# GLA groups of a hybrid scan layer: the products of both 64-channel heads side by side in the instruction order

## What is computed

```
def step(s, blk):                       # one chunk of 32 tokens
    qb, kb, vb, gb = blk
    b = jnp.cumsum(gb, axis=-2)
    b_last = b[..., -1:, :]
    q_dec = qb * jnp.exp(b)
    k_inv = kb * jnp.exp(-b)
    k_tail = kb * jnp.exp(b_last - b)
    att = jnp.where(lower_tri, jnp.einsum("bhik,bhjk->bhij", q_dec, k_inv), 0.0)
    o = jnp.einsum("bhij,bhjv->bhiv", att, vb) + jnp.einsum("bhik,bhkv->bhiv", q_dec, s)
    s_new = jnp.swapaxes(jnp.exp(b_last), -1, -2) * s + jnp.einsum("bhjk,bhjv->bhkv", k_tail, vb)
    return s_new, o
```

## Time and profile before

| | |
|---|---|
| median of 3 runs | 1610.77 us (1608.57 to 1614.6) |
| profiled execution, its own time | 1610.87 us |
| its span, first to last instruction | 1609.1 us |
| PE busy | 1465.1 us, 91% of the span |
| DVE, ACT, POOL busy | 704.9, 513.9, 85.3 us |
| mean granted clock of TensorE | 0.959 of full speed |
| DMA | 178.09 MB, mean 111 GB/s |

### The profile page before, as it was taken

How to read it: one execution, slowest core, us unless ns; L and a number is a source line. 1 busy time by engine, 2 the same in 40 slices (tenths; PEclk the granted TensorE clock), 3 DMA queues, 4 the chain that set the end, 5 groups by cost and what they waited for, 6 DMA issues and landing times.

```text
span 1609.1 us, 18385 instructions
## 1 busy us (share of the span) xinstructions
PE 1465.1 (91%) x7701; PEld 1191.7 (74%) x7701; DVE 704.9 (44%) x891; ACT 513.9 (32%) x715; POOL 85.3 (5%) x90
## 2 busy tenths in 40 slices
PE   3589999999999998999999999998776999999994
PEld 1377777777779998777777677887565887888883
DVE  2324333333335784553154436666673333423245
ACT  2233421122212545434243325555233222122220
POOL 3100000000000000000011101110000000000000
PEclk9999999999999999999989799999887999999997
DMA  9525446555434664550111101213421332333221
GB/s 297 188 79 157 151 151 185 175 162 159 150 125 126 169 177 122 165 183 17 40 53 40 27 27 40 53 53 105 131 79 51 107 99 86 92 105 91 86 73 52
DMA packets 201937, 178.09 MB, mean 111 GB/s; under 512 B 6642, under 2 KB 166912, under 8 KB 201856
## 3 DMA queue, kind: packets, MB, share of 16 engines
q1 hardware_dynamic: 192000, 139.14, 29.9%
q0 software_dynamic: 9856, 37.78, 7.1%
HBM read 174.81 MB, written 2.10 MB: 110 GB/s over the span
## 4 chain that ended last, share of the span: by engine, by line
PE 83%; DVE 7%; ACT 5%; issue 4%; DMA 1%; POOL 1%; SPq 0%; ACTq 0%; DVEq 0%; POOLq 0%
PE ps L1524 24%; PE ps L1525 23%; PE ps L1526 23%; PE ps L1548 2%; PE ps L1806 2%; ACT w_hi L648 1%; PE ps L1838 1%; PE ps L1836 1%; ACT hfull L664 1%; DVE w_lo L1034 1%; PE ps L1564 1%; PE ps L1555 1%; DVE stats L1049 1%; PE ps L1809 1%; PE ps L1821 1%
## 5 line engine op out<-in xcount | busy, mean ns | idle before, releaser
L1524 PE MATMUL ps<-h_hi,w_lo 128*128 128x512 f32 (+2 forms) x1136 | 403.5, 355 | 21.3 <-DVE h_lo L1069 16.2
L1034 DVE TENSOR_TENSOR w_lo<-w_raw,w_hi 128x2048 fp32r<-128x2048 f32 (+3 forms) x113 | 250.5, 2219 | 379.5 <-ACT w_hi L648 379.3
L1525 PE MATMUL ps<-h_lo,w_hi 128*128 128x512 f32 (+2 forms) x1136 | 398.1, 350 | 0.0
L1526 PE MATMUL ps<-h_hi,w_hi 128*128 128x512 f32 (+2 forms) x1136 | 397.7, 350 | 0.0
L648 ACT ACTIVATE w_hi<-w_raw 128x2048 fp32r<-128x2048 f32 (+3 forms) x113 | 209.5, 1855 | 547.5 <-PE ps L1526 546.3
L1524 PEld LDWEIGHTS ps<-h_hi,w_lo 128*128 128x128 f32 (+1 forms) x1136 | 217.7, 192 | 60.1 <-DVE h_lo L1069 17.2
L1526 PEld LDWEIGHTS ps<-h_hi,w_hi 128*128 128x128 f32 (+1 forms) x1136 | 217.2, 191 | 30.3
L1525 PEld LDWEIGHTS ps<-h_lo,w_hi 128*128 128x128 f32 (+1 forms) x1136 | 217.7, 192 | 28.6
L1524 PE MATMUL ps<-h_hi,half_lo 128*128 128x512 f32 (+1 forms) x272 | 108.1, 398 | 3.3 <-DVE gate L1377 3.3
L1525 PE MATMUL ps<-h_lo,half_hi 128*128 128x512 f32 (+1 forms) x272 | 103.7, 381 | 0.0
L1526 PE MATMUL ps<-h_hi,half_hi 128*128 128x512 f32 (+1 forms) x272 | 103.2, 379 | 0.0
(11 more groups left out here) (198 smaller groups left out, 1901.9 us busy)
## 6 DMA issues: line engine op xcount, KB each, us to landing
w_raw<-ffn_w_in SPq DMA_DIRECT2D x132, 512.0 KB, 5.3
ada_block<-w_ada POOLq DMA_DIRECT2D x36, 1024.0 KB, 6.0
w_raw<-ffn_w_out SPq DMA_DIRECT2D x60, 512.0 KB, 4.1
half_raw<-w_mix_in SPq DMA_DIRECT2D x48, 256.0 KB, 3.3
w_raw<-w_mix_out SPq DMA_DIRECT2D x12, 512.0 KB, 4.8
w_raw<-w_mix_in SPq DMA_DIRECT2D x8, 512.0 KB, 4.2
w_raw<-ffn_w_out SPq DMA_DIRECT2D x12, 256.0 KB, 3.9
xl<-x SPq DMA_DIRECT2D x4, 512.0 KB, 11.1
```

What stands on the lines that cost most here:

```text
L1034: nc.vector.tensor_tensor(lo, raw, hi.bitcast(F32), ALU.subtract).then_inc(s_lo[s], 1)
L1524: nc.tensor.matmul(dst, s_low, m_high, start=start, stop=False)
L1525: nc.tensor.matmul(dst, s_high, m_low, start=False, stop=False)
L1526: return nc.tensor.matmul(dst, s_high, m_high, start=False, stop=stop)
```

## The change

For GLA groups, a function `attention_pair` takes the place of the two calls of `attention`. It goes tile by tile: the KINV product of head one, that of head two, the 64x64 product of head one, that of head two. `updates` exchanges its two loops, so that the heads alternate there too (for HGRN groups, with one head, it stays what it was). `attention_pair` stands directly ahead of `updates`, after the dense products that used to stand between the first head's attention and the updates. On DVE the first head's mask moves behind `tails` (direction 0) or behind `scans` (direction 1).

```diff
+            def attention_pair(g, d):
+                (hd, _, _), _ = heads_of(g)
+                pe.wait_ge(s_qdec, n2(g, d))
+                pe.wait_ge(s_kinv, n2(g, d))
+                pe.wait_ge(s_tail, n2(g, d))
+                pe.wait_ge(s_kt, n2(g, d))
+                pe.wait_ge(s_am, max(ATT[g, d, hd] - 1, 0))
+                a0, b0 = (0, HALF) if d == 0 else (HALF, 0)
+                for tile in range(TL):
+                    c = tile * P
+                    for hd, p0, pn in heads_of(g):
+                        nc.tensor.matmul(ps[:, att_bank(g, hd), c:c + P], KINV[d][p0:p0 + pn, c:c + P],
+                                         QDEC[d][p0:p0 + pn, c:c + P], start=True, stop=True, skip_group_check=True)
+                    for hd, p0, pn in heads_of(g):
+                        ins = nc.tensor.matmul(ps[a0:a0 + HALF, att_bank(g, hd), c + b0:c + b0 + HALF],
+                                               TAILX[d][p0:p0 + pn, c + a0:c + a0 + HALF],
+                                               QDEC[d][p0:p0 + pn, c + b0:c + b0 + HALF], start=True, stop=True,
+                                               skip_group_check=True)
+                        if tile == TL - 1:
+                            ins.then_inc(s_att, 1)
...
             def updates(g, d):
                 pe.wait_ge(s_kt, n2(g, d))
-                for hd, p0, pn in heads_of(g):
-                    v = slice(hd * P, (hd + 1) * P)
-                    for j in range(5):
+                for j in range(5):
...
+                    for hd, p0, pn in heads_of(g):
+                        v = slice(hd * P, (hd + 1) * P)
...
                 turn_tails(g, 0)
-                attention(g, 0, first)
+                if not gla:
+                    attention(g, 0, first)
                 if gla_next:
                     dense(nxt, "gate0")
                 else:
                     dense_lat(nxt, "f0")
+                if gla:
+                    attention_pair(g, 0)
                 updates(g, 0)
-                if gla:
-                    attention(g, 0, second)
...
                     turn_tails(g, 1)
-                    attention(g, 1, first)
                     gla_z(nxt, 0)
                     dense(nxt, "gate1")
+                    attention_pair(g, 1)
                     updates(g, 1)
-                    attention(g, 1, second)
                     gla_z(nxt, 1)
```

More of the change, by code:

```diff
@@ L1410, in _ @@
                     forget(g, 1)
-                mask(g, 0, first)
+                if not gla:
+                    mask(g, 0, first)
                 scans(g, 1)
@@ L1416, in _ @@
                 decayed(g, 1)
-                states(g, 0)
-                tails(g, 1)
+                if gla:
+                    tails(g, 1)
+                    mask(g, 0, first)
+                    states(g, 0)
+                else:
+                    states(g, 0)
+                    tails(g, 1)
                 if gla_next:
@@ L1431, in _ @@
                     forget(nxt, 0)
-                mask(g, 1, first)
+                if not gla:
+                    mask(g, 1, first)
                 if gla_next:
@@ L1812, in attention @@
                 ins.then_inc(s_att, 1)
+            def attention_pair(g, d):
[18 more added lines that the diff above has]
+                            ins.then_inc(s_att, 1)
             def updates(g, d):
                 pe.wait_ge(s_kt, n2(g, d))
-                for hd, p0, pn in heads_of(g):
-                    v = slice(hd * P, (hd + 1) * P)
-                    for j in range(5):
-                        slot = 0 if j < 2 else j - 1
-                        tile = j if j < 2 else TC + order(d)[j - 2]
+                for j in range(5):
+                    slot = 0 if j < 2 else j - 1
+                    tile = j if j < 2 else TC + order(d)[j - 2]
+                    for hd, p0, pn in heads_of(g):
+                        v = slice(hd * P, (hd + 1) * P)
                         ins = nc.tensor.matmul(ps[p0:p0 + pn, 5, slot * P:(slot + 1) * P], ktok[:, j, p0:p0 + pn],
@@ L1892, in _ @@
                 turn_tails(g, 1)
-                attention(g, 1, first)
                 if gla:
                     dense(nxt, "gate0", 4, KT)
+                    attention_pair(g, 1)
                 else:
+                    attention(g, 1, first)
                     dense(nxt, "gate0")
                 updates(g, 1)
-                if gla:
-                    attention(g, 1, second)
                 dense_lat(nxt, "f1")
```

## The result

The changed kernel's profiled execution took 1587.66 us and a second one 1586.83. Two more, at 2391 and 3593 us, are left out, and nothing like them came back in four later executions of the same kernel, 1584.8 to 1587.5. Against the kernel before the ratio is **0.9861, 95% interval 0.9828 to 0.9894**. Measured again, over four executions, it was 1586.51 us and 0.9862 (0.9848 to 0.9877). The span fell from 1609.1 to 1585.9 us, by 23.2.

The account below looks back on a forecast made before the run. PE's own list was taken to bound the kernel. Attention 10.7, updates 2.8 and clock 4.8, less 1.8 at the fourth place, gave 16.5 us off 1610.87: 1594 us, range 1587 to 1604.

Parts of the forecast that it names:

- PE bounds, its own list decides: Whole kernel: PE is busy 91% of the span, so time is won on PE's own list or not at all.
- Attention, 10.7 us: GLA attention, four places: both heads' row halves work at once, a pair takes 2.68 us, 10.7 us go.
- rival 2: GLA pairs: matmuls start and end in program order, a tile takes 0.83 us; 1597 us in all, chance 10%.
- Updates, 2.8 us: GLA updates, four places: with heads alternating, 1.95 us become 1.24, so 2.8 us go; bounds 2.0 to 2.8.
- The fourth place, 1.8 us back: Group 0, direction 1: PE waits 2.7 us for DVE's second mask instead of 0.92; 1.8 us back, bounds 0 and 2.
- The clock, 4.8 us: Blocks behind the four places: three falls go, gla_z's stays, one comes elsewhere; 4.8 us won, bounds 9.5 won, 2 lost.
- A sign that I had named: First readouts: the prediction is wrong if one waits for mask or states at any place but the fourth.
- The slower rival: Four places: halves exclude each other, long narrow stretches draw the clock down; 10 us more, 1620 us, chance 4%.

Follow-up runs that it names:

- e5: The changed kernel with each pair's KINV products of both heads first, then the 64x64 products, heads still alternating; 1584.2 us, ratio 0.9849.
- e3: The changed kernel with heads one behind the other, each doing four KINV products, then four 64x64 products; 1590.4 us, ratio 0.9882.
- e2: The changed kernel with the loops of updates as before the change, heads outside; 1589.6 us, ratio 0.9875.
- e7: The changed kernel with pairs, HGRN attention and each readout ordered by form; 1564.4 us, ratio 0.9726.
- e8: e7 with the second head's mask moved ahead of decayed and tails on DVE at group 0, direction 1; 1559.2 us, ratio 0.9680.
- e1: The changed kernel, but in the pair's place head one does all four tiles, then head two; 1607.2 us, ratio 0.9983.
- e10: The kernel before, with only each GLA head's attention doing four KINV products, then four 64x64 products; 1592.1 us, ratio 0.9891.
- e4: The changed kernel with the pair directly behind the transposes, ahead of the dense products, at all four places; 1603.8 us, ratio 0.9959.

## Why the prediction was right, and what was off

- **PE bounds, its own list decides.** Right for what was won, which is all on PE, in products or in clock. What was lost, 0.9 and 1.1 us, are waits of PE for DVE.
- **Attention, 10.7 us.** Measured 11.0, of which 0.45 was one run at clock 0.50. The pair took 2.73 us, the predicted 2.7. The assumption drawn from the updates' records, that row halves work at once as column halves do, is shown by e5: 16 records in the time of 8. The reason given for the size, changes of form, is shown by e3: 0.165 us each on average. (For the 64x64 pair the prediction took 0.15 "by the same ratio"; that ratio gives 0.12, and a pace of half the 0.22 us gives 0.14. Nothing hangs on it, since only the sum over both forms was measured.)
- **Program order** (rival 2). A pair in which the second head's product can begin only with the first head's second record was worked out at 3.3 us. The pairs took 2.73 us, and all four records of a tile's KINV products stand in one row of 0.42 us. So the trace does not agree with the rule of the Trainium skill (TensorE: Matmul & The Clock Gate, part 3) that matmuls start and end in program order.
- **Updates, 2.8 us.** Measured 2.84 in the trace, and 2.8 again in e2's.
- **The fourth place, 1.8 us back.** The mechanism was right, but only 0.9 us came (0.74 for the mask, 0.17 for the states): the clock fell in the first readout, which gave DVE more time; that is the way to the prediction's lower bound of 0. e7 shows the term in full once the readout is fast, 3.6 us of wait, and e8 takes it away.
- **The clock, 4.8 us: this term was mis-sized.** In the stretch costed the trace has 8.1 us in dense blocks, 0.7 in gla_z and 0.45 in an attention, 9.3 in all, close to the term's far bound (9.5). I had kept the fall at gla_z and added one fall elsewhere; both were wrong, as all four blocks ran at 1.00. And 2.9 us more came from the first HGRN attention, behind the last place that I costed; I had looked at no block there. The wait for the states behind it took 1.1 of them back. That this is luck in part is shown by e5, whose clock fell at that place again. The step that failed is the one that kept one fall, took 1.5 off for another and costed nothing behind the last place.
- **A sign that I had named came, outside the four places.** I had said that I am wrong if a first readout waits for mask or states anywhere but at the fourth place. At the other three places none does, but the first HGRN readout waits 1.1 us for the states, since PE gets there earlier and DVE does not.
- The sum, 16.5, against 23.2: attention gave 0.3 more, the fourth place 1.1 (0.7 lost instead of 1.8), dense blocks and gla_z 4.0 (8.8 instead of 4.8), the HGRN place 2.9, and 1.6 went the other way (1.4 of it in the stretch with the new wait), which makes the 6.7 between them.
- **The slower rival** (narrow products long enough to draw the clock down) did not come in the change, but its mechanism is real: it is what e1 shows. Its price was on the high side: 10 us of clock in e1, against the 20 that I had worked out.

Not settled: what exactly draws the clock down. The runs say where it fell and where not, and that both the length of the narrow stretch (e1, e10) and what stands ahead of it (e4) count. Neither is enough: e5 and the changed kernel have the same instructions from the last GLA updates to the first HGRN attention and its dense block, and the clock fell there in e5 and not in the changed kernel. No run changed one thing with all else fixed in time, and the places move from kernel to kernel. So that the new order keeps the clock up by itself is not shown; what is shown is that it stayed up, at all four places, through the dense block and the pair in every run that has the pair behind the dense block.

## What to carry to other kernels

Where small products of two shapes alternate, put all of one shape first: a change of shape cost 0.165 us here, and ordering by shape gave 17 us to the old kernel (e10; 8 of them are the products, most of the others the clock) and 22 to the changed one (e7) with no other edit. Products that use different halves of the array should stand next to each other, with dense products on both sides, and the stretch of narrow ones should be short, since in e1 the clock cost as much as the products that were added. Then look again at what the old delay had covered: a wait of 0.9 us for a mask became 3.6 us, and a readout that had not waited for its states now waits 1.1 us.

## What the runs showed of the hardware

- Products of two row halves of the array, written alternately, run at once at full pace: 16 records in 1.10 us, 8 in 1.08. The second half costs 0.013 us per tile.
- The clock fell to 1.2 GHz in stretches in which PE was busy for 100% of the time, with products of 64 rows (836 to 839 us before, 842 to 848 in e1). The stretch of `mean_squares`, 3.7 us with half of it idle, does not decide it: in the kernel before the clock fell 2.7 us behind it (904.72 to 908.43, the fall at 911.1), and in the changed kernel and in e10, with the same stretch, it stayed at 1.00 through the dense block that follows. Idle time is not shown to be without effect either: behind e7's wait of 3.6 us eight records took 2.00 us, at clock 0.50, and behind e8's wait of 0.9 us the same eight took 1.16.
- Where and how often the clock falls moves a kernel by several us without any work having changed: e5's fall behind its last GLA place cost 2.9 us in attention and dense block, of which 1.1 came back as a wait that was no longer there.
